# A hybrid network's expert stage: second half written out, modulation tiles dropped in its last layer and used five units earlier in its first

## What is computed

```
def hybrid_layer_2(x, c_act, ..., w_ada, b_ada, ..., peer_wq, peer_sub_keys, peer_down, peer_up):
    mod = (c_act @ w_ada + b_ada)[:, None, :]
    sh1, sc1, g1, sh2, sc2, g2 = jnp.split(mod, 6, axis=-1)
    h = rms_norm_2(x, norm1_g) * (1 + sc1) + sh1
    ...
    x = x + g1 * (merged @ w_out)
    ...
    h2 = rms_norm_2(x, norm2_g) * (1 + sc2) + sh2
    x = x + g2 * peer_ffn(h2, peer_wq, peer_sub_keys, peer_down, peer_up)

def second_block(x, c, ...):
    c_act = jax.nn.silu(c)
    for l in range(DEPTH):            # DEPTH = 2
        x = hybrid_layer_2(x, c_act, ..., w_ada[l], ...)
```

## Time and profile before

| | us |
|---|---|
| three runs, median (lowest to highest) | 3487.81 (3484.42 to 3490.41) |
| the profiled execution, its own time | 3485.6 |
| its span in the trace | 3483.9 |
| PE busy in the span | 2996.3 (86%) |
| first half, up to the mixer of layer 0 | 0 to 1264 |
| expert stage of layer 0, first load to last matmul | 1436 to 2362 |
| mixer of layer 1, first load to the expert stage's first load | 2376 to 2546 |
| expert stage of layer 1 | 2546 to 3473 |

### The profile page before, as it was taken

The page is one execution under the profiler, slowest core; times in us unless marked ns, Lnnn a source line. Parts: engine busy times, 40 slices in busy tenths (PEclk is TensorE's granted clock), DMA queues, the critical chain, the costliest instruction groups (busy, mean ns, idle before and its releaser), DMA issues. The chain is left out here.

```text
span 3483.9 us, 47780 instructions
## 1 busy us (share of the span) xinstructions
PE 2996.3 (86%) x17972; PEld 2639.4 (76%) x17972; DVE 2359.4 (68%) x4199; ACT 1492.4 (43%) x2252; POOL 440.4 (13%) x249
## 2 busy tenths in 40 slices
PE   6877998688799957799789899995779989989998
PEld 5776876677587746699789877774679979977776
DVE  5996676499767645496975565665469596656665
ACT  3324533232353333355654444443344574444443
POOL 0100000000000001389000000000059700000000
PEclk9998999899899987899999999997789999999999
DMA  5443444444344442356236566664146515666665
GB/s 197 145 157 139 188 177 171 162 147 153 137 181 187 166 159 81 112 176 187 61 126 207 201 223 235 224 228 152 38 154 187 158 49 167 218 206 223 239 215 178
DMA packets 135647, 584.78 MB, mean 168 GB/s; under 512 B 16187, under 2 KB 20060, under 8 KB 109916
## 3 DMA queue, kind: packets, MB, share of 16 engines
q1 hardware_dynamic: 134396, 576.86, 48.2%
q10 hardware_dynamic: 1008, 4.72, 0.3%
HBM read 573.06 MB, written 9.51 MB: 167 GB/s over the span
## 5 line engine op out<-in xcount | busy, mean ns | idle before, releaser
L2094 DVE TENSOR_TENSOR e_lo<-e_raw,e_hi 128x1024 fp32r<-128x1024 f32 x394 | 482.2, 1224 | 376.4 <-ACT e_hi L1918 373.5
L1918 ACT ACTIVATE e_hi<-e_raw 128x1024 fp32r<-128x1024 f32 x544 | 574.0, 1055 | 322.3 <-DMA e_raw<-up 196.9
L1836 PE MATMUL e_ps<-k_hhi,e_hi 128*128 128x256 f32 x2304 | 653.3, 284 | 44.1 <-POOL e_lo L1821 29.5
L1836 PE MATMUL e_ps<-k_hlo,e_hi 128*128 128x256 f32 x2304 | 646.7, 281 | 0.0
L1836 PE MATMUL e_ps<-k_hhi,e_lo 128*128 128x256 f32 x2304 | 646.1, 280 | 0.0
L725 DVE TENSOR_TENSOR f_wlo<-f_raw,f_whi 128x2048 fp32r<-128x2048 f32 x156 | 356.7, 2291 | 189.0 <-ACT f_whi L558 189.0
L1836 PEld LDWEIGHTS e_ps<-k_hhi,e_hi 128*128 128x128 f32 x2304 | 436.4, 189 | 48.7 <-POOL e_lo L1821 30.3
L558 ACT ACTIVATE f_whi<-f_raw 128x2048 fp32r<-128x2048 f32 x156 | 296.2, 1912 | 372.6 <-DMA f_raw<-ws 275.9
L1836 PEld LDWEIGHTS e_ps<-k_hlo,e_hi 128*128 128x128 f32 x2304 | 435.9, 189 | 0.0
L1836 PEld LDWEIGHTS e_ps<-k_hhi,e_lo 128*128 128x128 f32 x2304 | 435.2, 189 | 0.0
L1821 POOL TENSOR_TENSOR e_lo<-e_raw,e_hi 128x1024 fp32r<-128x1024 f32 x150 | 385.3, 2583 | 90.0 <-ACT e_hi L1918 89.1
(11 more groups left out here) (335 smaller groups left out, 5135.9 us busy)
## 6 DMA issues: line engine op xcount, KB each, us to landing
f_raw<-ws SPq DMA_DIRECT2D x156, 1024.0 KB, 5.7
e_raw<-down SPq DMA_DIRECT2D x288, 512.0 KB, 4.1
e_raw<-up SPq DMA_DIRECT2D x256, 512.0 KB, 4.8
e_ada<-ada SPq DMA_DIRECT2D x96, 512.0 KB, 3.7
f_x<-ada SPq DMA_DIRECT2D x48, 512.0 KB, 3.7
s_raw<-ws SPq DMA_DIRECT2D x24, 1024.0 KB, 4.9
f_x<-out SPq DMA_DIRECT2D x4, 1024.0 KB, 6.5
f_const<-consts SPq DMA_DIRECT2D x2, 1104.0 KB, 7.3
```

Of the source, the lines that this page charges most:

```text
L1836: last = nc.tensor.matmul(psD(n), w, h, start=kt == 0 and i == 0, stop=kt == KT - 1 and i == 2)
L1918: nc.scalar.activation(hi[:, i % RING, :], raw[:, i % RING, :], ACT.Copy).then_inc(S["hi_ready"], 1)
L2094: V.tensor_tensor(lo[:, i % RING, :], raw[:, i % RING, :], hi[:, i % RING, :].bitcast(F32), ALU.subtract).then_inc(S["lo_dve"], 1)
```

## The change

It does three things. The loop over the second half's layers is written out in Python, so that each layer has its own instructions, constants for addresses instead of registers, and its own names for buffers and semaphores (`tag`, `str(l)`). In the last layer's expert stage no modulation tile is loaded or multiplied, and `c_row` and the stored vector go too. In the other layer DVE asks for the tile of unit n + 3 instead of n - 2. Line numbers after it are one higher from L2104 on (L2103 becomes L2104, L2113 L2114, L2094 L2095).

```diff
@@ second_mixer, peer: arenas, PSUM tensors and semaphores get str(l) behind their names
-    pb = arena(nc, env["base"])
+    pb = arena(nc, env["base"], str(l))
...
@@ peer, SP
                 for i in range(RING, NU):
-                    if i == ADA_UNIT:
+                    if i == ADA_UNIT and l < DEPTH - 1:
                         sp.wait_ge(S["staged_mult"], 1)
                         sp.dma_start(c_row[:, :], inp["c_row"]).then_inc(S["in_crow"], 16)
-                    a = next_mod(i)
+                    a = next_mod(i) if l < DEPTH - 1 else None
...
-                sp.wait_ge(S["ada_done"], MODS)
-                for half in range(2):
-                    sp.dma_start(inp["mod_cols"][2 + half, :, :], modn[:, half * HALF_MOD:(half + 1) * HALF_MOD]).then_inc(S["out_mod"], 16)
-                sp.wait_ge(S["out_mod"], 32)
+                if l < DEPTH - 1:
+                    sp.wait_ge(S["ada_done"], MODS)
+                    for half in range(2):
+                        sp.dma_start(inp["mod_cols"][2 + half, :, :], modn[:, half * HALF_MOD:(half + 1) * HALF_MOD]).then_inc(S["out_mod"], 16)
+                    sp.wait_ge(S["out_mod"], 32)
@@ peer, DVE
                 def modulation(i):
-                    a = next_mod(i)
+                    a = next_mod(i) if l < DEPTH - 1 else None
...
                 for n in range(first, ND):
                     weigh(n)
                     rest(n + RING)
-                    modulation(n - 2)
+                    modulation(n + 3)
...
                     rest(ND + x + RING)
-                    modulation(ND + x - 2)
+                    modulation(ND + x + 3)
@@ program
-    with nc.Fori(0, DEPTH) as l:
+    for l in range(DEPTH):
         second_mixer(nc, env, l, inp)
         peer(nc, env, l, inp)
```

More of the change, by code:

```diff
@@ L177, in link, with arena @@
         self.wait()
-def arena(nc, base):
+def arena(nc, base, tag=""):
     at = [base]
@@ L190, in place @@
             at[0] += (size + 31) // 32 * 32
-        return nc.alloc_sbuf_tensor_at(name, shape, dtype, offset=offset)
+        return nc.alloc_sbuf_tensor_at(name + tag, shape, dtype, offset=offset)
     place.at = at
@@ L1165, in second_mixer @@
     with ExitStack() as cx:
-        psA = cx.enter_context(nc.psum_tensor("s_psA", [P, 4, CH], F32))
-        psS = cx.enter_context(nc.psum_tensor("s_psS", [P, 4, CH], F32))
+        psA = cx.enter_context(nc.psum_tensor("s_psA" + str(l), [P, 4, CH], F32))
+        psS = cx.enter_context(nc.psum_tensor("s_psS" + str(l), [P, 4, CH], F32))
         names = """in_x in_par in_bias raw0 raw1 hi_ready lo_ready unit_done acc_read small_ready small_read
@@ L1172, in second_mixer @@
             x_done out_x g1_ready""".split()
-        S = {n: cx.enter_context(nc.semaphore("s_" + n)) for n in names}
+        S = {n: cx.enter_context(nc.semaphore("s_" + n + str(l))) for n in names}
         raw_in = [S["raw0"], S["raw1"]]
@@ L1736, in peer @@
     gate = pb("e_gate", [P, D], offset=A_at + 16384)
-    late = arena(nc, A_at + FIRST * T * 4)
+    late = arena(nc, A_at + FIRST * T * 4, str(l))
     keys = late("e_keys", [P, 16, NE])
@@ L1756, in peer @@
     with ExitStack() as cx:
-        ps = cx.enter_context(nc.psum_tensor("e_ps", [P, 8, CH], F32))
+        ps = cx.enter_context(nc.psum_tensor("e_ps" + str(l), [P, 8, CH], F32))
         names = """in_const in_keys raw0 raw1 raw2 in_x out_x hi_ready lo_pool lo_dve unit_done psd_read score_mm sc_copied
@@ L1760, in peer @@
             staged_mult weighted g_hi_ready g_lo_ready gate_mm gate_ready prod_done x_done in_crow in_ada ada_done out_mod""".split()
-        S = {n: cx.enter_context(nc.semaphore("e_" + n)) for n in names}
+        S = {n: cx.enter_context(nc.semaphore("e_" + n + str(l))) for n in names}
         raw_in = [S["raw0"], S["raw1"], S["raw2"]]
```

## The result

The changed kernel takes 3387.23 us (median of four runs, 3385.14 to 3389.63), the one before 3486.11 (four runs, 3483.07 to 3490.41): 98.9 us less, a ratio of 0.9716 with a 95% interval of 0.9699 to 0.9733.

What follows compares the result with a forecast made beforehand. PE idles in the expert stages because SP's loads queue behind waits for tile multiplies. Layer 0 42.1, layer 1 47.7 and loop turn 3 give 92.8, less 5 is 87.8 us: 3400 us, range 3391 to 3425.

Steps and rivals of the forecast that it cites:

- SP's wait for the multiply: Load queue in both expert stages: SP waited 92 times, 416.8 us in all, for tile multiplies, leaving PE idle.
- the clean paces: Expert stages: 2.83 us per down unit and 2.75 per up unit, taken for the whole stretches once SP stops waiting.
- both turns: PE's idle time from down to up half, 8.0 us before: 3.5 us gained in layer 0, 4.9 in layer 1.
- leaving out the tiles: Layer 1: dropping 48 loads, 48 multiplies and the final stores was worth nothing in itself; only the same wait counted.
- a sign of being wrong: Layer 1's up units at a pace of 2.80 us or more with PE full would show the prediction wrong.
- I take off 3 us in layer 0 ... and 2 in layer 1.: Allowance against the summed gain for late load landings: in layer 0 with the multiply, in layer 1 at stretch starts.
- With 1.9 us idle, falls in layer 0 as before.: PE's clock at layer 0's down-to-up turn: falls, so the first up unit still takes 5.3 us and gains nothing.
- all favourable bounds of the sum: Best case: nothing taken off and the clock kept in layer 0's turn (2.5 us), 95.3 us gained, so 3392.
- The register instructions: Instructions ahead of each load, removed by writing out the loop: 0.1 us beside a wait, unseen by PE, worth nothing.
- One reading: Load of unit 157, layer 0: issued behind a tile, 3.2 us after it could have been.
- the transfer itself: Rival: tiles sharing the DMA engines with loads make the idle time; layer 0 gains nothing, 3437 us; chance 0.09.
- stood for a tile: Rival: DVE waits for tiles landing late, holding up all rests; slower, 3555 us at 11.5 us landings; chance 0.03.

Runs made afterwards that it cites:

- e1: The changed kernel with layer 0's tiles used five units later again (unit n - 2 instead of n + 3); 3422.09 us, ratio 0.982.
- e2: The kernel before with only the tiles used earlier (unit n + 3), loop and layer 1's tiles kept; 3393.77 us, later 3395.10 us.
- e9: The changed kernel with layer 1's 48 tiles kept, loop written out, tiles used early; 3384.22 us, ratio 0.9701.
- e6: The changed kernel with layer 0's tile of unit n - 1 used instead of n + 3; 3387.43 us, ratio 0.9720.
- a0: The changed kernel itself measured once more, nothing changed; 3385.25 us, ratio 0.9708.
- e4: The changed kernel with 91 extra tile-sized transfers in layer 1, without multiplies, ahead of every second unit from unit 91; 3389.98 us, ratio 0.9723.
- e5: The changed kernel with layer 0's tile of unit n used instead of n + 3; 3385.77 us, ratio 0.9718.
- e3: The kernel before with only the loop written out, both layers' tiles used late; 3464.07 us, ratio 0.9940.
- e7: The changed kernel with the first two weighted rests moved ahead in DVE's queue; 3376.56 us, run again 3384.49 us.

## Why the prediction missed by a little

Its cause, its places and nearly all its sizes held. SP's wait for the multiply made the idle time (e1, e2); the clean paces of 2.83 and 2.75 us, read from 8 and 11 units, held over 362 units of two layers; both turns came within 0.3 us; leaving out the tiles was worth nothing in itself (e9: 1.2 us, the multiply in layer 1's turn, as worked out).

One of these was luck. The up pace of 2.75 us was read in layer 0 and used for layer 1 too, where the trace of the kernel before shows 2.80 us for the last six units, PE full as well:

```profile
3456.40:3473.20 16.80, 16.80 (x73) 13.35 (x71) 8.08 (x11) 5.93 (x9) 0.00 (x0) 1.00 0.24 78
```

The prediction doesn't speak of it, except as a sign of being wrong. Had the changed kernel shown that pace throughout layer 1, as e6 did, the time would have been 6.8 us longer, 3394, and inside the range.

The measured time is 12.8 us below the 3400, and three steps of the prediction failed, all of size and all to one side.

- *"I take off 3 us in layer 0 ... and 2 in layer 1."* Nothing had to come off. The allowance was for late landings, and its basis was the landing times of the kernel before, up to 8.1 us. The changed kernel shows 150.0 us for the down half of each layer and 349.3 and 349.0 us for the up units behind the first: the clean paces with nothing added. Many of the old landings were long because of the very wait that went. Behind it SP often issued the tile and two loads within 1.1 us (29 of 48 cases in each layer), and they landed after 3.7, 4.4 and 5.8 us in the median; ahead of unit 91 of layer 0, where no tile is, the median was 3.7. I priced the new regime with a quantity that the old regime had made. But bunching isn't all of it: in layer 1 of the changed kernel, without a tile, the median from unit 91 on was 4.3 us, and 3.5 in a0, the same program. What holds in both is that none of it reached PE.
- *"With 1.9 us idle, falls in layer 0 as before."* The idle time was 1.72 us and the clock stayed at 1.00, in this turn and in all nine others with 1.73 us idle (e2, e4, e5, e9 and a0): 2.4 us. No row stood behind this step; the up half of layer 1 before had the clock staying behind 2.14 us idle, which spoke against it.
- *The range.* Its lower end took all favourable bounds of the sum (3392) and left 1 us for everything that the change doesn't touch. The start of the expert stage's first matmul, in layer 0, lies anywhere from 1438.0 to 1448.9 us in fourteen traces of code that hardly differs there, and whole stretches of matmuls run at one of two paces. 2.2 us of the 98.1 came from outside the stretches. Another 2.5 are the distance of the median from the profiled execution, which I had put at 2.2 above and which was 0.3 below. With the 5 and the 2.4 these make 12.1 of the 12.8 us. For a kernel whose own runs spread by 5 to 7 us the range needed as much below the sum's best case.

The register instructions were costed at nothing because PE doesn't see them. That holds where SP isn't late: layer 1 of e2, with them, has the stretches of e9 to 0.8 us. With SP late, e3 has the two expert stages 8 us shorter without them, which doesn't bear on the sum. The gains of the parts overlap: alone, the written-out loop gives 20 us and the earlier use 90; together they give 104 (e9), and with the tiles of layer 1 gone as well 99 and 103 (the changed kernel and a0).

One reading was loose: in the earlier trace rows it is the tile that went out 3.2 us after the buffer came free, and the load behind it 3.7 (2012.56). Nothing in the sum used it.

Of the rivals, the transfer itself is refuted (e2, e4, e9). DVE never stood for a tile: in the changed kernel each load issued behind a tile landed 1.2 to 4.8 us after it. In the traces of the kernel before, the changed one and e9 the tile, issued first, landed first in 240 of 240 cases. The Trainium skill ("DMA: Bandwidth & Descriptors", Queues, rings and completion order) gives no promise of that; here nothing hung on it.

## What to carry to other kernels

A queue that serves both a critical stream and a side stream passes the side stream's waits on to the critical one. Count, in steps of each engine's own program, when the release comes and when the queue asks: here the loss was nothing with the release in time, under 2 us with it one step later, and 35 to 40 with two. Dropping the useless work was worth what it blocked and 1.2 us more. And when a wait is removed, price what remains with durations from stretches that never had it, and look at more than one such stretch: here the ends of the two layers ran at different paces.

## What the runs showed of the hardware that I had not expected

With PE full and the granted clock at 1.00, a long stretch of matmuls runs at one of two paces and mostly keeps it. For 256 columns the starts are 118 or 113 ns apart (2.83 or 2.72 us per down unit), for 512 columns the mean is 229 or 233 ns (2.75 or 2.80 us per up unit). The pace changed between two traces of one program (e7, e2), and was the slow one for all 127 up units of a layer in e4 and e6. In the second trace of e2 it changed within the up half of layer 1, from 2.75 to 2.80 us behind one unit of 2.92, with PE full. It is worth up to 6.8 us per stretch. What sets it stays open: the DMA share doesn't (0.78 and 0.56 with the same slow pace), and none of the runs varies anything else that would tell.

PE's idle time alone doesn't tell whether the clock falls. In the up half of the kernel before it stayed at the upper level behind idle times of up to 2.14 us, and fell behind one of 2.05 and one of 2.92 us; the first of these cost the unit behind it 1.7 us. In layer 1 of e3 it fell behind 1.86 us and stayed behind 2.79.
